# Odd-layer output projection in tile pairs with seven block products

## The reference

```python
u = silu(layernorm(u, ln_g, ln_b))
y = (u * silu(g)) @ w_out              # (2048, 1024) @ (1024, 1024)
x = x + gate * rmsnorm(y, post_g)      # y * rsqrt(mean(y*y) + eps) * post_g
```

## Time and profile before

| what | us |
|---|---|
| median of 3 runs (2303.71 to 2305.51) | 2303.99 |
| the profiled execution | 2304.18 |
| its span in the trace | 2302.3 |
| first matmul of the odd output | 2093.43 |
| last matmul of the program begins | 2293.63 |

### The profile page before, as it was taken

The page is one execution under the profiler, slowest core; times in us unless marked ns, Lnnn a source line. Parts: engine busy times, 40 slices in busy tenths (PEclk is TensorE's granted clock), DMA queues, the critical chain, the costliest instruction groups (busy, mean ns, idle before and its releaser), DMA issues. The chain is left out here.

```text
span 2302.3 us, 30998 instructions
## 1 busy us (share of the span) xinstructions
PE 2239.1 (97%) x11298; PEld 1882.7 (82%) x11298; DVE 1371.0 (60%) x2086; ACT 1127.4 (49%) x2100; POOL 883.5 (38%) x660
## 2 busy tenths in 40 slices
PE   6999998999999999999999989999999999999998
PEld 5888888898897788888888878887888888888887
DVE  8333336343436776767677641116999999994443
ACT  5555534222224555555555545556555566654433
POOL 4222222232222111101101023232899999992454
PEclk9999999999999999999999999999999999999999
DMA  8533323434344122222131333331111211145553
GB/s 305 183 137 137 137 78 141 166 131 141 136 149 146 51 66 68 65 69 65 33 83 33 99 112 120 127 119 38 46 55 42 68 56 42 64 157 167 164 166 108
DMA packets 151730, 245.75 MB, mean 107 GB/s; under 512 B 9012, under 2 KB 95284, under 8 KB 147254
## 3 DMA queue, kind: packets, MB, share of 16 engines
q1 hardware_dynamic: 146564, 235.31, 31.0%
q10 hardware_dynamic: 5042, 8.81, 1.0%
HBM read 157.84 MB, written 86.25 MB: 106 GB/s over the span
## 5 line engine op out<-in xcount | busy, mean ns | idle before, releaser
L2428 POOL TENSOR_TENSOR conv_g<-conv_g,product 128x1024 f32<-128x1024 f32 x160 | 385.1, 2408 | 34.2 <-ACT product L2477 24.5
L2572 DVE SCALAR_TENSOR_TENSOR ps_b<-u,cols,ps_b 128x1024 f32<-128x1024 f32 x304 | 391.7, 1288 | 9.2
L2688 PE MATMUL ps_a<-ho_hi,wp_lo 128*128 128x512 f32 x768 | 300.8, 392 | 5.6 <-DVE h_left L2628 5.6
L2690 PE MATMUL ps_a<-ho_hi,wp_hi 128*128 128x512 f32 x768 | 300.2, 391 | 0.0
L2689 PE MATMUL ps_a<-h_left,wp_hi 128*128 128x512 f32 x768 | 299.9, 390 | 0.0
L2477 ACT ACTIVATE product<-u,cols 128x1024 f32<-128x1024 f32 x160 | 183.3, 1151 | 170.1 <-POOL conv_g L2428 168.8
L1789 DVE TENSOR_TENSOR pt_lo<-ps_pt,pt_hi 128x512 fp32r<-128x512 f32 x256 | 176.2, 689 | 135.8 <-ACT pt_hi L1684 133.7
L1684 ACT ACTIVATE pt_hi<-ps_pt 128x512 fp32r<-128x512 f32 x256 | 154.1, 603 | 203.2 <-PE ps_pt L1876 202.3
L1779 DVE TENSOR_REDUCE mx<-ps_s 128x1 f32<-128x512 f32 x248 | 168.3, 684 | 34.3 <-PE ps_s L1868 32.6
L1677 ACT ACTIVATE probs<-ps_s,bias 128x512 f32<-128x512 f32 x248 | 168.7, 700 | 17.6 <-DVE bias L1785 9.3
L2688 PEld LDWEIGHTS ps_a<-ho_hi,wp_lo 128*128 128x128 f32 x768 | 144.8, 189 | 37.2 <-DVE h_left L2628 7.5
(11 more groups left out here) (453 smaller groups left out, 5414.6 us busy)
## 6 DMA issues: line engine op xcount, KB each, us to landing
scratch_ret_pack<-pack SPq DMA_DIRECT2D x14, 1280.0 KB, 5.5
pack<-scratch_ret_pack SPq DMA_DIRECT2D x14, 1280.0 KB, 6.2
ada<-in_ada_w_dram SPq DMA_DIRECT2D x16, 768.0 KB, 6.1
wp_raw<-in_od_w_in_dram SPq DMA_DIRECT2D x24, 512.0 KB, 3.7
xt<-in_x_dram SPq DMA_DIRECT2D x16, 512.0 KB, 6.6
mix_e<-scratch_mix SPq DMA_DIRECT2D x16, 512.0 KB, 4.3
x_e<-in_x_dram SPq DMA_DIRECT2D x16, 512.0 KB, 4.9
scratch_x<-mod_acc SPq DMA_DIRECT2D x16, 512.0 KB, 3.0
```

The source lines that it names most:

```text
L2428: pool.tensor_tensor(half(conv_g, h), half(conv_g, h), product[adds(c, i, h) % 2][:], ALU.add).then_inc(added, 1)
L2572: dve.scalar_tensor_tensor(acc[h], units(c, k, h), params(c, k), acc[h], ALU.mult, ALU.add).then_inc(tap, 1)
L2688: pe.matmul(dst, lo[:, k, :], h_hi[:, k, t], start=k == 0, stop=False)
L2690: mm = pe.matmul(dst, hi[:, k, :], h_hi[:, k, t], start=False, stop=k == KD - 1)
```

## The change

**Odd output.** Tiles 0 to 3 are computed as before, though written out and in a new order. Tiles 4 to 15 are taken in six pairs. A pair is a product of a 256-row by a 1024x1024 matrix, seen as 2x2 blocks: A11, A12 (halves of the first tile's operand), A21, A22 (of the second) against four quarters of the weight. Instead of eight block products seven are made (M1 to M7, 12 matmuls each), by the scheme of Strassen in Winograd's form. It needs four sums of operand blocks (S1 to S4), four sums of weight quarters (T1 to T4) and seven sums of the products (U2, U3, U4 and the results C11, C12, C22, C21), which VectorE writes to SBUF in `res`. So the scaling by the root mean square (`scaled`, L3149 in the new file) now reads SBUF where it read PSUM.

**Even output.** The four weight sums are formed there, in eight pieces: SyncE loads four blocks of 128x256 of the next layer's weight, GpSimd does four dependent additions after the residual sum of tiles 2 to 9 (`sum_piece`), and SyncE stores them to a new scratch array `w_sums`. The odd output loads them (four loads of 1 MB), and ScalarE and VectorE split them into high and low parts. SyncE's and GpSimd's loops of the even output are written out.

The core of the diff (declarations, and parts of it that read as the ones shown, are left out):

```diff
+            def sum_piece(i):
+                a, b, c, d = pieces[i % 2]
+                pool.wait_ge(piece_in[i % 2], 64 * (i // 2) + 64)
+                pool.tensor_tensor(c, c, b, ALU.subtract).then_inc(piece_sum, 1)
+                pool.wait_ge(piece_sum, 4 * i + 1)
+                pool.tensor_tensor(b, b, a, ALU.subtract).then_inc(piece_sum, 1)
+                pool.wait_ge(piece_sum, 4 * i + 2)
+                pool.tensor_tensor(a, a, c, ALU.add).then_inc(piece_sum, 1)
+                pool.wait_ge(piece_sum, 4 * i + 3)
+                pool.tensor_tensor(d, d, a, ALU.subtract).then_inc(piece_sum, 1)
...
         @block.scalar
...
+            for q in pairs:
+                n = q + 1
+                act.wait_ge(part_done, parts(q, M1))
+                if q > FIRST:
+                    act.wait_ge(c_step, combined(q - 1, C11))
+                act.activation(o.m1[:], X, ACT.Copy).then_inc(m1_kept, 1)
+                if n <= LAST:
+                    activate(2 * n, 2 * q - 1 if q > FIRST else 2 * q)
+                if q > FIRST:
+                    act.wait_ge(n_turned, min(2 * n, NT - 1) + 1 if n <= LAST else NT)
+                    square(2 * q - 1, res[1][:], c_step, combined(q - 1, C21), nt[:])
+                if n <= LAST:
+                    activate(2 * n + 1, 2 * q)
+                    operand_hi(n, A11)
+                    operand_hi(n, A12)
+                    act.wait_ge(m_done, 2 * n + 2)
+                act.wait_ge(c_step, combined(q, C11))
+                square(2 * q, res[0][:], c_step, combined(q, C12))
+                if n <= LAST:
+                    for a in (S2, S1, S3, S4, A22):
+                        operand_hi(n, a)
...
         @block.gpsimd
...
+            deviation(2)
+            multiply(1)
+            rstd(0)
+            add(0)
+            deviation(3)
+            multiply(2)
+            rstd(1)
+            deviation(4)
+            add(1)
+            multiply(3)
+            deviation(5)
+            multiply(4)
+            rstd(2)
+            add(2)
+            multiply(5)
+            deviation(6)
+            rstd(3)
+            add(3)
+            for q in pairs:
+                n = q + 1
+                if q > FIRST:
+                    add(2 * q - 2)
+                    rstd(2 * q - 1)
+                if n <= LAST:
+                    deviation(2 * n + 1)
+                    multiply(2 * n)
+                if n < LAST:
+                    deviation(2 * n + 2)
+                if q > FIRST:
+                    add(2 * q - 1)
+                if n <= LAST:
+                    multiply(2 * n + 1)
+                rstd(2 * q)
...
         @block.vector
...
+            def operand_sum(q, a):
+                one, two = place(2 * q), place(2 * q + 1)
...
+                if a == S1:
+                    dve.wait_ge(m_done, 2 * q + 2)
+                    ins = dve.tensor_tensor(op_raw[S1], two[:, first, :], two[:, last, :], ALU.add)
...
+            def combine(q, c):
...
+                if c == U2:
+                    dve.wait_ge(part_done, parts(q, M6))
+                    dve.wait_ge(m1_kept, q - FIRST + 1)
+                    if q == FIRST:
+                        dve.wait_ge(res_done, PLAIN)
+                    ins = dve.tensor_tensor(u2, o.m1[:], Y, ALU.add)
...
+                elif c == C22:
+                    dve.wait_ge(c_step, combined(q, U3))
+                    dve.wait_ge(res_stored[1], 16 * q)
+                    ins = dve.tensor_tensor(right[1], u3, PB, ALU.add)
...
+            for q in pairs:
+                n = q + 1
+                if q > FIRST:
+                    scaled(2 * q - 2)
+                combine(q, U2)
+                if n <= LAST:
+                    moments(2 * n + 1)
+                operand_lo(q, S4)
+                operand_lo(q, A22)
+                if n <= LAST:
+                    normed(2 * n + 1)
+                if q > FIRST:
+                    scaled(2 * q - 1)
+                else:
+                    weight_lo(T4)
+                combine(q, U3)
+                if n < LAST:
+                    moments(2 * n + 2)
+                combine(q, U4)
+                if n <= LAST:
+                    operand_lo(n, A11)
+                combine(q, C11)
+                if n < LAST:
+                    normed(2 * n + 2)
+                if n <= LAST:
+                    operand_lo(n, A12)
+                combine(q, C12)
+                combine(q, C22)
+                if n <= LAST:
+                    for a in (S1, S2, S4):
+                        operand_sum(n, a)
+                    operand_lo(n, S2)
+                    operand_sum(n, S3)
+                    operand_lo(n, S1)
+                combine(q, C21)
+                if n <= LAST:
+                    operand_lo(n, S3)
...
         @block.tensor
...
+            turn_n(4)
+            turn_v(5)
+            for k in range(KD):
+                mm = product(2, 1, k)
+            mm.then_inc(y_done, 1)
+            turn_n(5)
...
+            for q in pairs:
+                n = q + 1
+                if q == FIRST:
+                    pe.wait_ge(yn_done, PLAIN - 1)
+                else:
+                    pe.wait_ge(c_step, combined(q - 1, C11))
+                with_weight(q, M1, A11, X, 0, 0)
+                if n <= LAST:
+                    turn_n(2 * n)
+                if q > FIRST:
+                    pe.wait_ge(c_step, combined(q - 1, C12))
+                with_sum(q, M6, S2, Y, T2)
+                if n <= LAST:
+                    turn_v(2 * n + 1)
+                if q == FIRST:
+                    pe.wait_ge(yn_done, PLAIN)
+                else:
+                    pe.wait_ge(c_step, combined(q - 1, C22))
+                with_sum(q, M5, S1, PB, T1)
+                if q > FIRST:
+                    pe.wait_ge(c_step, combined(q - 1, C21))
+                with_sum(q, M7, S3, Z, T3)
+                if n <= LAST:
+                    turn_n(2 * n + 1)
+                if n < LAST:
+                    turn_v(2 * n + 2)
+                pe.wait_ge(m1_kept, q - FIRST + 1)
+                with_weight(q, M2, A12, X, 1, 0)
+                pe.wait_ge(c_step, combined(q, U2))
+                with_weight(q, M3, S4, Y, 1, 1)
+                pe.wait_ge(c_step, combined(q, U3))
+                with_sum(q, M4, A22, Z, T4)
```

More of the change, by code:

```diff
@@ L1950, in even_out, with piece_of @@
         mods = high.take("mods_e", [P, 2 * KD])
+        PIECES, PN = KD, BANK // 2
+        B11, B12, B22, B21 = range(4)
+        piece0, piece1 = low.take("piece0", [P, 4, PN]), low.take("piece1", [P, 1, PN])
+        piece2 = high.take("piece2", [P, 3, PN])
+        pieces = [[piece0[:, i, :] for i in range(4)], [piece1[:, 0, :]] + [piece2[:, i, :] for i in range(3)]]
+        piece_in = [sem(f"piece_in{i}") for i in range(2)]
+        piece_sum = sem("piece_sum")
+        piece_stored = [sem(f"piece_stored{i}") for i in range(2)]
+        def piece_of(w, i, b):
+            rows, columns = ((0, 0), (0, 1), (1, 1), (1, 0))[b]
+            r, c = (rows * KD // 2 + i // 2) * P, columns * BANK + i % 2 * PN
+            return w[r:r + P, c:c + PN]
         x1 = [acc[:, i * D:(i + 1) * D] for i in range(2)]
@@ L2723, in odd_tiles @@
     o.rv = small.take("rv_o", [P, 2])
-    o.ssy, o.msy, o.ry, o.ssh, o.part = [small.take(f"{n}_o", [P, 1]) for n in ("ssy", "msy", "ry", "ssh", "part")]
+    o.ssy, o.msy, o.ry, o.ssh, o.part, o.last = [small.take(f"{n}_o", [P, 1]) for n in ("ssy", "msy", "ry", "ssh", "part", "last")]
     o.ps_v, o.ps_n = ps_b[:, 0:D], ps_b[:, D:2 * D]
@@ new lines, in _ @@
+            for t in range(2):
+                activate(t + 1, t)
+                split(t + 1)
+                if t == 1:
+                    weight_hi(T2)
+                square(t, ps_y[t % 2], y_done, t + 1)
+            activate(3, 2)
+            split(3)
+            weight_hi(T1)
+            activate(4, 2)
+            weight_hi(T3)
+            act.wait_ge(m_done, 5)
+            square(2, ps_y[0], y_done, 3)
+            operand_hi(FIRST, A11)
+            operand_hi(FIRST, A12)
+            activate(5, 3)
@@ new lines, in _ @@
+            for t in range(2):
+                moments(t + 2)
+                normed(t + 2)
+                split(t + 1)
+                if t == 1:
+                    weight_lo(T2)
+                scaled(t)
+            moments(4)
+            normed(4)
+            split(3)
+            moments(5)
+            normed(5)
+            weight_lo(T1)
+            scaled(2)
+            operand_lo(FIRST, A11)
+            operand_lo(FIRST, A12)
+            moments(6)
+            for a in (S1, S2, S4):
+                operand_sum(FIRST, a)
@@ new lines, in part @@
+            def part(q, m, a, dst, b_hi, b_lo):
+                pe.wait_ge(alo_done, 7 * (q - FIRST) + a + 1)
+                for k in range(HK):
+                    hi, lo = op_hi[a][:, k, :], op_lo[a][:, k, :]
```

(4 more changed lines are left out.)

488 lines of the change are left out of this document (334 added, 154 removed).

## The result

The changed kernel took 2308.07 us (median of 15 runs, 2305.49 to 2311.85), the kernel before 2305.03 us (15 runs on the same chip, 2300.05 to 2309.16). The ratio is 1.0017, with a 95% interval of 1.001 to 1.0024: about 4 us slower (the two medians are 3.0 us apart). In a second set of runs, beside runs of the kernel before of its own, it came out as 1.002 (1.0011 to 1.0029). The prediction was 2308.0 us.

What follows compares the result with a forecast made beforehand. A chain through all engines, with holds and a store wait, was taken to bound pairs at 25.0 us, not TensorE's 22.56. -16.3 + 8.6 + 8.5 + 0.3 + 2.9 + 0.3 = +4.3 on 2304.18 gave 2308.5, so 2308; range 2293 to 2318.

Steps and rivals of the forecast that it cites:

- Matmuls saved: Odd output's pairs: 84 matmuls for 96, six pairs, 16.3 us less if TensorE stays the pace; 22.56 us a pair.
- The way in: Tiles 2 to 7, ahead of the pairs: `turn_n(7)` starts 8.6 us later than TensorE alone would have it.
- (a): On the way in, `turn_n(5)` after tile 2 waits 2.2 us for normalising, behind `multiply(3)`, high and low part, and statistics.
- (c): On the way in, U2 needs `add(3)`; statistics, roots and normalising of tile 7 follow, so TensorE waits 2.1 us.
- (b): On the way in, M5 of the first pair waits 3.0 us for tile 3 scaled, behind squares late in ScalarE's list.
- The periods: Tile pairs (6, 7) to (14, 15): one period of 23.75 and three of 25.0 us, 8.5 us of waiting.
- The last pair: The last pair of the odd output has no layer norm beside it: 0.3 us of waiting.
- The end: After the last matmul, GpSimd's `add(14)` goes first and holds VectorE's scaling 2.4 us: 2.9 us more; 0.5 if VectorE is first.
- The even output: Four additions delay GpSimd's root 1.9 to 2.2 us against 2.16 us of slack: 0.3 us in all, bounds 0 to 2.4.
- TensorE keeps the pace: Rival: holds and store wait do not add up, loop 22.1 us, under 22.56; change -9.2, 2295 us; chance 0.34.
- Holding multiplies: Rival: VectorE held 2.4 us more per pair on the loop, period 27.4, four periods +9.6, 2318 us; chance 0.19.
- The clock: Rival: TensorE's clock halves after waits of about 2.3 us, 1.5 us each, up to 6; part of the slower range.

Runs made afterwards that it cites:

- x_small: Changed kernel with GpSimd's multiplies (tile 5 on) and additions (tile 4 on) cut to the first 128 of 1024 columns; ratio 0.9979 to the kernel before.
- x_third: Changed kernel with a third result buffer, so C22 no longer waits for the store of the odd tile before; ratio 1.0011 to the kernel before.
- x_after: The changed kernel once more, without any edit; ratio 1.002 to the kernel before.
- x_warm: Changed kernel with 20 transposes of a constant on TensorE in its wait before the turn of tile 7; last matmul at 201.06 us, one run.

## Why the prediction was right

The number is nearer than the method allows: 2308.07 for 2308 is partly luck. The forecast change was +4.3 us on the profiled execution, the medians differ by 3.0 and the ratio says 3.9; and the kernel before, taken as 2303.99 from three runs, has a median of 2305.03 over fifteen. What was right is the mechanism. Point by point, by its own steps; measured values are those of the profile after.

- **Matmuls saved, -16.3.** As said; but TensorE's own pace is 22.95 us a pair (x_small), not 22.56: four turns cost 3.9 us with their changeovers, not 3.5. This changes nothing where the chain sets the period.
- **The way in, +8.6.** The start of the turn is met; the split into waits is not, and how long TensorE alone would take was not measured. The turn of tile 7 starts 74.08 us after the stage's first matmul; the text had 74.1 (2167.5 - 2093.43). (a) gave 2.00 us for 2.2, (c) 2.35 for 2.1. (b) gave 1.21 for 3.0: M5 starts at the same point (65.96, and 65.95 in x_third, where the wait is 2.75), only TensorE arrives later, for the clock had fallen after (a) (granted 0.58 in 4 us from 2140.43 on, 1.00 in x_third's same stretch).
- **The periods, +8.5.** 23.67, 25.36, 24.77, 24.80 = 98.60 us for 98.75. The scaling is held (2.12 us for 2.1), and in pairs 4 and 5 C22 waits for the store (2.08 and 2.11 us). The second period is no proof of the walk: there C22 waits for no store, and the held low part of A11 (2.83 us), which the walk had slipping in, takes its place; that the size fits there is luck (in x_after that period does have the store wait, and is 25.13). That TensorE would wait "mostly before `turn_n(2n+1)`" was wrong: M6 and the turn wait 0.8 to 0.9 us each, less than the 1 to 2 us named as a sign. Shown: without GpSimd's length all waits go (x_small), without the store wait 0.9 us a pair (x_third).
- **The last pair, +0.3.** It was 0.9: its M6 waits 0.91 us like all others. Of the terms of the sum this one is off the most, by 0.6 us.
- **The end, +2.9.** 3.0 measured, by the mechanism named: GpSimd first by 0.06 us.
- **The even output, +0.3.** 0.0 in the profile. The transfers are 4 MB each way, not the 1 MB of the text, and cost nothing that can be seen either.
- **Sum.** +1.6 in the stage and +3.0 at the end are +4.6 for +4.3; the ratios 1.0017 and 1.002 are +3.9 and +4.6 us.

Of the rivals, "TensorE keeps the pace" needed the holds gone; x_small is that world. It is 9.6 us faster than the changed kernel, but only 4.8 us faster than the kernel before (ratio 0.9979), where the rival had 9.2: the way in and TensorE's own 22.95 us a pair stay. "Holding multiplies" priced a double hold at 27.4 us; a further hold of 2.1 us occurred (A11, 2.83 us for 0.69), but it took the place of the store wait. The clock stayed within what was allowed for: 0.75 us by x_warm, for 1.5 set for a wait.

What stays open: why the low clock at the entry of the even output lasts some 3 us in one execution and some 10 in another of the same code, and whether a wait of some 2 us is followed by one at all: the 2.0 us before the turn of tile 5 were in the changed kernel and were not in x_third.

## To carry to other kernels

Saving work on the engine that sets the pace pays only until the loop through the other engines closes; here their busy sums (13 to 19.8 of 22.56 us) said "fits", and only the walk through each engine's list, with holds between VectorE and GpSimd and the store's landing, gave 25.0 us a pair (24.8 measured, where TensorE's own pace is 22.95). Where two delays stand side by side (a hold and a store wait), removing one shows what the other leaves, and a fifth of a microsecond in who comes first changes which is paid. Before moving an operation, ask what its output buffer and its input buffer hold up, and which transfers stand behind its store.

## Not expected of the hardware

- One-column roots on GpSimd took 0.55 us alone and up to 1.07 us beside VectorE's operations with two SBUF inputs.
- In the one execution of x_warm the filled wait kept the clock: 20 transposes (2.34 us) in place of 2.35 us of idling, clock 1.00 for 0.58 in the 4 us that follow.
- Executions of the same code differed by up to 6.3 us at the first turn of the even output (1374.4 to 1380.7 us over 13 profiles on several chips; up to 3.7 us on one), while the 200 us of the odd output repeated to 0.1 us (201.81 and 201.92, and 200.20 and 200.21 for the old one). A difference of two spans must be cut at such marks before it is put down to a change.
